# The v and o blocks of an mLSTM layer by Strassen's seven products, and x with the first weights in contiguous parts

## What is computed

```python
h = rmsnorm(x, norm1_g[l])
z = jnp.einsum('bsd,de->bse', h, w_in[l])
q_a, k_a, v_a, x_m, v_m, o_m, i_pre, f_pre = jnp.split(z, IN_SPLITS, axis=-1)
...                       # attention of q_a, k_a, v_a; convolution of x_m; mLSTM with v_m; sigmoid(o_m) as its gate
x = x + jnp.einsum('bse,ed->bsd', mixed, w_out[l])
x = x + moe_ffn(rmsnorm(x, norm2_g[l]), ...)   # every expert: [1024 x 2048], SwiGLU, [1024 x 1024]
```

## Time and profile before

| | us |
|---|---|
| median of 3 runs | 1050.03 (1049.18 to 1050.25) |
| the profiled execution | 1048.32 |
| its span, first to last instruction | 1046.5 |
| TensorE busy in the span | 1031.7 |
| VectorE busy | 199.1 |
| ScalarE busy | 143.0 |
| GpSimd busy | 4.1 |
| mean load rate over the span | 407 GB/s |

### The profile page before, as it was taken

The page is one execution under the profiler, slowest core; times in us unless marked ns, Lnnn a source line. Parts: engine busy times, 40 slices in busy tenths (PEclk is TensorE's granted clock), DMA queues, the critical chain, the costliest instruction groups (busy, mean ns, idle before and its releaser), DMA issues.

```text
span 1046.5 us, 11612 instructions
## 1 busy us (share of the span) xinstructions
PE 1031.7 (99%) x4797; PEld 385.9 (37%) x4797; DVE 199.1 (19%) x506; ACT 143.0 (14%) x301; POOL 4.1 (0%) x20
## 2 busy tenths in 40 slices
PE   8999999999999999999999999999999999999998
PEld 4655543333333333333333333333333333333333
DVE  1263232111111111111111111111111111111111
ACT  2144431100111100100111111111101100011101
POOL 0000000000000000000000000000000000000000
PEclk9999999999999999999999999999999999999999
DMA  9954799999999999999999999999999999999997
GB/s 341 428 217 161 292 364 406 427 428 434 432 429 431 431 432 431 433 431 432 433 431 432 430 433 431 432 431 432 435 431 433 430 432 425 431 426 427 424 425 292
DMA packets 24313, 425.87 MB, mean 407 GB/s; under 512 B 2912, under 2 KB 3424, under 8 KB 6368
## 3 DMA queue, kind: packets, MB, share of 16 engines
q1 hardware_dynamic: 23856, 424.96, 95.6%
q10 hardware_dynamic: 432, 0.55, 0.1%
HBM read 424.45 MB, written 1.05 MB: 407 GB/s over the span
## 4 chain that ended last, share of the span: by engine, by line
PE 87%; DMA 8%; SPq 5%; another core or an unknown queue 0%; DVE 0%; issue 0%; ACT 0%
PE bank L1607 38%; PE bank L1642 18%; PE bank L1211 6%; PE bank L1519 5%; PE bank L1569 5%; DMA ring<-in_w_gate_up 5%; SPq L422 3%; PE bank L1404 3%; PE bank L1457 3%; PE bank L1530 2%; DMA ring<-in_w_down 2%; PE bank L1627 2%; PE bank L1249 1%; DMA ring<-in_w_in 1%; PE bank L1618 1%; SPq L567 0%
## 5 line engine op out<-in xcount | busy, mean ns | idle before, releaser
L1607 PE MATMUL bank<-ring,xe_t 128*64 128x512 f32 x2048 | 447.9, 594 | 5.1 <-DMA ring<-in_w_gate_up 4.6
L1607 PEld LDWEIGHTS bank<-ring,xe_t 128*64 128x64 f32 x2048 | 143.8, 137 | 305.6 <-issue 293.8
L1642 PE MATMUL bank<-ring,late 128*64 128x512 f32 x992 | 219.9, 596 | 0.0
L1642 PEld LDWEIGHTS bank<-ring,late 128*64 128x64 f32 x992 | 68.4, 137 | 127.3 <-issue 122.0
L1144 DVE TENSOR_SCALAR gate_c<-bank 128x512 f32<-128x512 f32 x32 | 22.2, 692 | 432.1 <-PE bank L1607 432.1
L1211 PE MATMUL bank<-ring 128*128 128x512 f32 x160 | 73.5, 605 | 2.2 <-DVE ring L908 2.1
L810 ACT ACTIVATE s_sb<-bank 128x256 f32<-128x256 f32 x32 | 12.3, 384 | 454.8 <-PE bank L1618 454.8
L1569 PE MATMUL bank<-late,s_sb 64*128 64x512 f32 x248 | 61.6, 615 | 0.0
L1519 PE MATMUL bank<-xres,pick 128*64 128x512 f32 x248 | 60.1, 605 | 0.0
L826 ACT ACTIVATE late<-bank 128x512 f32<-128x512 f32 x31 | 18.5, 597 | 218.8 <-PE bank L1642 218.8
L1142 DVE COPY row_of<-fold 128x64 f32 x31 | 6.0, 195 | 197.0 <-PE bank L1457 197.0
(11 more groups left out here) (212 smaller groups left out, 421.2 us busy)
## 6 DMA issues: line engine op xcount, KB each, us to landing
ring<-in_w_gate_up SPq DMA_DIRECT2D x44, 4096.0 KB, 33.9
ring<-in_w_down SPq DMA_DIRECT2D x22, 4096.0 KB, 32.4
ring<-in_w_gate_up SPq DMA_DIRECT2D x36, 2048.0 KB, 32.9
ring<-in_w_down SPq DMA_DIRECT2D x15, 2048.0 KB, 11.7
ring<-in_w_in SPq DMA_DIRECT2D x5, 2048.0 KB, 22.3
ring<-in_w_gate_up SPq DMA_DIRECT2D x8, 1024.0 KB, 23.5
ring<-in_w_down SPq DMA_DIRECT2D x6, 1024.0 KB, 29.2
ring<-in_w_out SPq DMA_DIRECT2D x2, 2048.0 KB, 32.3
```

Source lines behind the costliest of these rows:

```text
L1607: mm = pe.matmul(bank[h][c * CAP:(c + 1) * CAP, :], xe_t[:, k, :], w[:, k % RUN, at:at + BANK], start=False, stop=(k == KD - 1), skip_grou ...
L1642: mm = pe.matmul(dst[c * CAP:(c + 1) * CAP, :], turned[:, at:at + CAP], w[:, k % DRUN, c * BANK:(c + 1) * BANK], start=(k == 0), stop=(k = ...
```

## The change

Both products of the filler become one: the tokens A (256 x 1024) times the v and o weights side by side, B (1024 x 1024), by Strassen's method. A and B are cut in 2 x 2 quarters (A: 128 x 512, B: 512 x 512), and seven quarter products of 4 matmuls each replace eight. VectorE makes four sums of A's quarters (`s_1` to `s_4`, 128 x 512 words), GpSimd four sums of B's quarters (`t_1` to `t_4`, 128 x 2048 words; `t_3` and `t_4` in place in the weights, `t_1` and `t_2` in slot 2 behind the x weights). The results are put together partly in PSUM (a product that starts with `start=False` adds to the one before) and partly by VectorE (`fill_added`, and one addition straight into `vm`). ScalarE's copies go from four to two. The fillers are 14 halves, placed by `FILL_AT`: 4, 4, 3 and 3 in the four passes, where it was 4 each.

The loads of slots 0, 2 and 1 for the experts now wait for `z_fill` 6 and 7, since slots 0, 1 and 2 are in use till then. The transposed tokens and block 0 of the weights come as one tensor, `first`, whose four parts are each contiguous in memory (x and weights of a k side by side, 3 KB a partition and k); they land in slots 5 and 6 and no longer in 9 and 0, so block 4 can be loaded into slot 0 without a wait. `attn_bias` and `w_out` are loaded later in SyncE's order.

```diff
-X_PARTS = ((0, 1), (1, 2), (2, 4), (4, KD))
+FIRST_PARTS = ((0, 1), (1, 2), (2, 4), (4, KD))
+FIRST_RUN = SEQ + HALF
+FILL_AT = (((0, 1), (2,), (3,)), ((4, 5), (6,), (7,)), ((8, 9), (10,), ()), ((11, 12), (13,), ()))
...
         sig_c = km_t
+        s_1 = in_second_half(4 * P).rearrange("p (k n) -> p k n", k=4)
+        s_2, s_3 = (qm_t[:, 2 * i:2 * i + 2, :].rearrange("p h (g n) -> p (h g) n", g=2) for i in range(2))
+        t_1, t_2 = (ring[:, 2 * PIECE + i * 4 * HALF:2 * PIECE + (i + 1) * 4 * HALF].rearrange("p (k n) -> p k n", k=4)
+                    for i in range(2))
+        b_11, b_21, b_12, b_22 = (win[:, c, 4 * r:4 * r + 4, :] for c in range(2) for r in range(2))
+        t_4, t_3 = b_11, b_12
...
-        xg = hn_flat.rearrange("p (k n) -> p k n", k=KD)
+        first_flat = ring[:, 5 * PIECE:5 * PIECE + KD * FIRST_RUN]
+        x_win = first_flat.rearrange("p (k n) -> p k n", k=KD)
+        xg, win_0 = x_win[:, :, 0:SEQ], x_win[:, :, SEQ:FIRST_RUN]
+        u_2 = hn_flat[:, HM * SW:T * D]
...
+        u_3 = ring[:, 9 * PIECE + T * D + 4 * SW:10 * PIECE]
...
+        a_11, a_12, a_21, a_22 = (ht[:, 4 * c:4 * c + 4, r * P:(r + 1) * P] for r in range(T) for c in range(2))
...
             def load_win(b):
-                sp.dma_start(win[:, b % WINS, :, :], w_in[b]).then_inc(ld_win[b], 16)
+                sp.dma_start(win[:, b % WINS, :, :], w_in[b - 1]).then_inc(ld_win[b], 16)
...
-            for i, (lo, hi) in enumerate(X_PARTS):
-                sp.dma_start(xg[:, lo:hi, :], x_t[:, lo:hi, :]).then_inc(ld_xt[i], 16)
-                sp.dma_start(win[:, 0, lo:hi, :], w_in[0, :, lo:hi, :]).then_inc(ld_xt[i] if i else ld_win[0], 16)
+            for i, (lo, hi) in enumerate(FIRST_PARTS):
+                rows = first[lo:hi].rearrange("k n -> (k n)").rearrange("(p n) -> p n", p=P)
+                sp.dma_start(first_flat[:, lo * FIRST_RUN:hi * FIRST_RUN], rows).then_inc(ld_first[i], 16)
...
+            sp.dma_start(wr_br, w_router).then_inc(ld_wr, 16)
+            load_win(4)
+            sp.wait_ge(z_q, 4)
+            load_win(5)
+            sp.wait_ge(h_ready, 2)
             sp.dma_start(bias_a, attn_bias).then_inc(ld_bias_a, 16)
-            sp.dma_start(wr_br, w_router).then_inc(ld_wr, 16)
...
-            for b in (4, 5):
-                sp.wait_ge(z_q, 2 * (b - WINS) + 2)
-                load_win(b)
-            for b, used, n in ((2, z_xm, 2), (3, z_v, 2), (0, z_fill, 2)):
-                sp.wait_ge(used, n)
-                load_gu(0, b, b)
-                if b == 2:
-                    for i in range(4):
-                        sp.dma_start(bgu[i * NE:(i + 1) * NE, :], b_gate_up[0, :, i * BANK:(i + 1) * BANK]).then_inc(ld_bgu, 16)
+            sp.wait_ge(z_v, 2)
+            load_gu(0, 3, 3)
+            for i in range(4):
+                sp.dma_start(bgu[i * NE:(i + 1) * NE, :], b_gate_up[0, :, i * BANK:(i + 1) * BANK]).then_inc(ld_bgu, 16)
...
-            sp.wait_ge(z_fill, 4)
+            sp.wait_ge(z_fill, 6)
+            load_gu(0, 0, 0)
+            load_gu(0, 2, 2)
+            sp.wait_ge(z_fill, 7)
...
+            for b in (4, 5):
+                pool.wait_ge(ld_win[b], 16)
+            pool.wait_ge(z_xm, 2)
+            pool.tensor_tensor(t_1, b_12, b_11, ALU.subtract).then_inc(t_ready, 1)
+            pool.wait_ge(t_ready, 1)
+            pool.tensor_tensor(t_2, b_22, t_1, ALU.subtract).then_inc(t_ready, 1)
+            pool.tensor_tensor(t_3, b_22, b_12, ALU.subtract).then_inc(t_ready, 1)
+            pool.wait_ge(t_ready, 2)
+            pool.wait_ge(z_fill, 1)
+            pool.tensor_tensor(t_4, b_21, t_2, ALU.subtract).then_inc(t_ready, 1)
...
             def filled(n):
-                act.wait_ge(z_fill, n + 1)
-                if n < 2:
-                    act.activation(vm[:, n, :, 0:DM], bank[n][:, :].rearrange("p (h n) -> p h n", h=HM),
+                if n == 0:
+                    act.wait_ge(z_fill, 1)
+                    act.activation(p_1, bank[0][:, :], ACT.Copy).then_inc(fill_read, 1)
+                if n == 1:
+                    act.wait_ge(z_fill, 3)
+                    act.activation(vm[:, 0, :, 0:DM], bank[0][:, :].rearrange("p (h n) -> p h n", h=HM),
                                    ACT.Copy).then_inc(fill_read, 1)
-                else:
-                    act.activation(om[:, n - 2, :], bank[n - 2][:, :], ACT.Copy).then_inc(fill_read, 1)
...
                                   bank[5][:, 0:SEQ].unsqueeze(1).broadcast_to([P, 4, SEQ]), ALU.mult).then_inc(h_ready, 1)
+            dve.wait_ge(h_ready, 2)
+            step(dve.tensor_tensor(s_1, a_21, a_22, ALU.add))
+            step(dve.tensor_tensor(s_3, a_11, a_21, ALU.subtract))
+            settle()
+            step(dve.tensor_tensor(s_2, s_1, a_11, ALU.subtract))
+            settle()
+            dve.tensor_tensor(s_4, a_12, s_2, ALU.subtract).then_inc(h_ready, 1)
...
+            def fill_added(out, held, product, b):
+                dve.wait_ge(z_fill, product)
+                dve.tensor_tensor(out, held, bank[b][:, :], ALU.add).then_inc(fill_sum, 1)
             for j in range(PAIRS):
+                if j == 1:
+                    dve.wait_ge(fill_read, 1)
+                    fill_added(u_2, p_1, 2, 1)
+                if j == 2:
+                    fill_added(u_3, p_1, 4, 1)
...
+                if j == PAIRS - 1:
+                    dve.wait_ge(z_fill, 6)
+                    dve.wait_ge(consts, 5)
+                    dve.tensor_tensor(vm[:, 1, :, 0:DM], p_1.rearrange("p (h n) -> p h n", h=HM),
+                                      bank[1][:, :].rearrange("p (h n) -> p h n", h=HM), ALU.add).then_inc(fill_sum, 1)
...
                 normalise(2 * j + 1)
+                if j == 2:
+                    dve.wait_ge(fill_sum, 2)
+                    fill_added(om[:, 1, :], u_3, 5, 0)
+                if j == PAIRS - 1:
+                    fill_added(om[:, 0, :], u_2, 7, 0)
...
                 for k in ks:
-                    mm = pe.matmul(dst[:, :], tokens[:, k, t * P:(t + 1) * P], win[:, b % WINS, k, :],
+                    mm = pe.matmul(dst[:, :], tokens[:, k, t * P:(t + 1) * P], win[:, b % WINS, k, :] if b else win_0[:, k, :],
...
-            pe.wait_ge(ld_win[0], 16)
-            for k in range(KD):
-                pe.wait_ge(x_norm, k + 1)
-                for t in range(T):
-                    mm = project(bank[t], 0, t, range(k, k + 1), xg)
-                    if k == KD - 1:
-                        mm.then_inc(z_q, 1)
+            for i, (lo, hi) in enumerate(FIRST_PARTS):
+                pe.wait_ge(ld_first[i], 16)
+                for k in range(lo, hi):
+                    pe.wait_ge(x_norm, k + 1)
+                    for t in range(T):
+                        mm = project(bank[t], 0, t, range(k, k + 1), xg)
+                        if k == KD - 1:
+                            mm.then_inc(z_q, 1)
...
+            fill_a = (a_11, s_2, a_12, s_3, s_1, a_22, s_4)
+            fill_b = (b_11, t_2, b_21, t_3, t_1, t_4, b_22)
+            fill_anew = (True, True, False, False, True, False, False)
...
-                b, t, q = 4 + i // 8, (i // 4) % 2, i % 4
+                n, q = i // 2, i % 2
                 if q == 0:
-                    if t == 0:
-                        pe.wait_ge(ld_win[b], 16)
-                    if b == 4:
-                        pe.wait_ge(v_read, t + 1)
-                    else:
-                        pe.wait_ge(fill_read, t + 1)
-                mm = project(bank[t], b, t, range(2 * q, 2 * q + 2))
-                if q == 3:
+                    if n == 0:
+                        pe.wait_ge(ld_win[4], 16)
+                        pe.wait_ge(v_read, 1)
+                    if n == 1:
+                        pe.wait_ge(v_read, 2)
+                        pe.wait_ge(h_ready, 3)
+                        pe.wait_ge(t_ready, 2)
+                    if n == 2:
+                        pe.wait_ge(fill_read, 1)
+                    if n == 3:
+                        pe.wait_ge(fill_sum, 1)
+                        pe.wait_ge(t_ready, 3)
+                    if n == 4:
+                        pe.wait_ge(fill_read, 2)
+                    if n == 5:
+                        pe.wait_ge(fill_sum, 2)
+                        pe.wait_ge(t_ready, 4)
+                    if n == 6:
+                        pe.wait_ge(fill_sum, 3)
+                for k in (2 * q, 2 * q + 1):
+                    mm = pe.matmul(bank[n % 2][:, :], fill_a[n][:, k, :], fill_b[n][:, k, :],
+                                   start=fill_anew[n] and k == 0, stop=(k == 3), skip_group_check=True)
+                if q:
...
                     pe.wait_ge(m_g, HM - 1 + h // 2)
-                    pe.wait_ge(fill_read, 3 + h // 2)
+                    if h == 0:
+                        pe.wait_ge(fill_read, 2)
+                        pe.wait_ge(fill_sum, 5)
...
                     attend(j - 1)
-                fill(4 * j)
-                fill(4 * j + 1)
```

(31 more changed lines are left out.)

## The result

The changed kernel takes 1057.44 us (median of 5 runs, 1056.47 to 1057.70), the kernel before, run beside it, 1049.18 us (5 runs, 1048.71 to 1050.25). The ratio is 1.0070, with a 95% interval of 1.0058 to 1.0082: slower by 8.3 us, where the forecast was a gain of 3.3. The profiled execution lasts 1057.51 us around a span of 1055.7.

What follows compares the result with a forecast made beforehand. The experts' load stream was taken to set the end, its start set by TensorE's line. First loads 2.4 plus seven products 1.9 minus GpSimd sums 1.0 gave 3.3 us, so 1046.7 us; range 1044.4 to 1056, the forecast's own 1045.2 to 1047.9.

Steps and rivals of the forecast that it cites:

- the cost of the sums on GpSimd: VectorE's convolution beside GpSimd's sums: slowed to end 3.8 us late, 2.9 hidden, so a cost of 1.0 us.
- VectorE keeps 62%: VectorE beside a running GpSimd sum: 0.09 us lost in 0.24 us of overlap, so it keeps 62% of its rate.
- the slack of 2.87: ScalarE's copies after the convolution end at 65.90 us, TensorE asks at 68.77: 2.87 us of lateness stays hidden.
- The port is held: Rival, chance 0.28: each GpSimd sum blocks VectorE's second input for its whole length, costing 8.7 us; 1054.4 us.
- Its other term: Within the held-port rival: t_4 catches normalise(1), 3.9 us late against 2.2 of slack, 1.7 us more.
- The first loads: Block 0 at the start: contiguous loads remove TensorE's gaps, gaining 2.4 us, bounds 0 and 2.6.
- Seven products: Fill stage: 28 matmuls instead of 32 save 3.44 us, less 1.5 us of waits, a gain of 1.9 us.
- both predicted waits: Pass 3, TensorE waiting behind VectorE's additions: 0.5 us at turn_p(6) and 1.0 us at m_sum(0).
- The moved loads: Slots 0, 2 and 1 loaded after z_fill 6 and 7: cost 0, the old pause pays, 1.9 us in hand.
- The 1-for-1 rule: Each microsecond by which TensorE reaches the first expert earlier moves the load stream and the end by as much.

Runs made afterwards that it cites:

- kept-busy kernel: The changed kernel with 36 unused products (72 records) on TensorE in its stall ahead of the gate columns; 1058.19 us, ratio 1.0088 to the kernel before.
- loads alone: The kernel before with only the contiguous first loads and the new place and load order that go with them, ordinary products, no weight sums; 1046.39 us, ratio 0.9973.
- sums early: The changed kernel with t_1 and t_2 made sooner in slot 10, t_3 after the gate rows, t_4 after a normalisation; 1045.92 us, ratio 0.9969 to before.
- kernel without sums: The changed kernel without GpSimd's four weight sums, its products reading unsummed weight quarters in the same number and order; 1045.73 us, ratio 0.9968 to before.
- reordered version: Sums early, with VectorE's two additions of pass 3 each moved one step later, behind what TensorE waits for; 1044.22 us, ratio 0.9949 to before.
- in parts: The changed kernel with each of its four GpSimd sums cut into four instructions of 512 elements; 1056.67 us, ratio 1.0066 to before.

## Why the prediction was wrong

**The step that failed** is the cost of the sums on GpSimd: "VectorE keeps 62%" and, from it, "Cost 1.0 us". The rate came from one copy of 0.29 us beside a select of 0.29 us, a pair too short to tell a share from a hold. In its place: the two engines take turns by whole instructions where both read SBUF. The convolution ended at 69.76 us, about 11.2 later than its old place shifted by the faster start (61.07 - 2.5), where the sum had 3.8. Less the slack of 2.87, which was right, that is the stall of 8.3 us for the forecast 1.0. The low clock behind it, some 3.6 us, had no term in the sum at all.

**The rival had the mechanism and not the size.** "The port is held" said 1054.4, 4.4 us slower than before; 8.3 were measured. That it is a port that is held, no run here shows; that VectorE is held for whole instructions, they do. It had one VectorE instruction let in between two sums, as the trace shows, and 3.9 us a sum; 4.5 were measured. Three sums of 0.6 more would have made its stall 7.0 + 1.8 = 8.8, where 8.3 were measured. What it lacked altogether is the clock behind the stall, 3.2 to 3.6 us. Its other term, 1.7 us for t_4 on normalise(1), is real (2.2 us in the kept-busy kernel) but did not show, since the low clock had moved t_4. And I gave it 0.28 for want of a row of two two-input instructions side by side. The rule that spoke for it, in "SBUF — State Buffer" of the Trainium skill, section "Who interferes with whom", is borne out by 3.17 us instead of 0.42; so are the 4.5 us for a sum of 2048 words of the "GPSIMD Engine Reference", section "Performance versus the Vector engine" (4.52).

**The first loads** were expected to give 2.4 us. The changed kernel's profile has 2.48, and alone they gave 2.3 by the medians (1048.73 - 1046.39). The spread starts at 25.7 to 28.1 us in the ten kernels with the new loads, 2.3 us earlier than 29.04 on average, so a single profile can be 1.3 us off here. The profile of loads alone is the latest of them, at 28.07.

**Seven products.** The mechanism is right: 28 products, and both predicted waits, at the predicted instructions (0.65 and 0.92 in the idle column, for 0.5 and 1.0). The gain was expected at 1.9 us. From the gate columns to the output product the kernel before takes 46.33 us and sums early 44.95: 1.4. The idle column hides part of the waits, since the end of a record is modelled. By the starts in the changed kernel, L1356 follows the filler of 112.04 by 2.53 us instead of four records of 0.43, 0.8 late, and L1429 (the `m_sum` of the changed kernel) follows the three turns of 117.99 (0.33) by 1.40, 1.1 late: 1.9 of waits, not 1.5.

**The moved loads** were costed at nothing. In the changed kernel TensorE was so late that this was no test. The kernel without sums has the same loads, and TensorE reaches the experts 3.1 us sooner than before; in sums early and the reordered version it does so 3.8 and 5.9 us sooner. In all three the end follows within about 1.4 us, so at most that much is theirs. The load rate speaks against it: without sums the old pause (180 and 90 GB/s at 142 to 146 us before) is nearly gone, at 349 and 276 GB/s in 140 to 144, but the dip where the first expert lets the next load go is still there (287 GB/s in 152 to 154, 197 in 156 to 158 before), so the loads ahead of it had landed. What the up to 1.4 us are stays open.

**The 1-for-1 rule**, that the end moves with the first expert, held to within about 1.4 us from profile to profile. That +8.25 in the profile stands beside +8.26 in the median is partly luck, since the spans of the same two profiles differ by 9.2.

## What to carry to other kernels

Before work goes to GpSimd "because it is idle", list what VectorE does in those microseconds with operands in SBUF, and count the two engines as one: the sum of their times, wherever they overlap. The price is then set by the moment and not by the amount; the same sums cost 11 us or nearly nothing (0.2 against no sums), with the first two six microseconds earlier and the third behind the gate rows. And a long stall of TensorE can cost more than its length: the ones of 7.6 to 8.4 us did, while a stall of 2.2 us in the kernel kept busy left the granted clock at 1.00.

## What was unexpected of the hardware

- **One-input instructions are held too.** The taps of L992 have one tensor input and went from 0.35 us each to 9.77 for four. Those that read PSUM were not held (0.48 us). The held ones read SBUF and are also faster, 0.35 us for 256 elements against 0.48 from PSUM; the trace cannot tell which of the two decides. "SBUF — State Buffer" of the Trainium skill, same section, has this case: a tensor_scalar in a mode that uses both ports contends. The trace agrees in that they were held, and normalise(1), 4.87 us for two, is a second case; the mode itself it does not show.
- **Turns are strict.** One VectorE instruction passed between two GpSimd ones, whether these took 4.5 us or, in parts, about 1.2 (16.12 us for twelve with VectorE's between them).
- **The clock's tail.** TensorE idle from about 66.3 to 74.6 us had a granted clock of 0.58 in 68 to 70, 0.50 from 70 to 82, and 1.00 after, with TensorE at work again since 74.6. Kept busy with unused products it stayed at 1.00, and 3.2 to 3.5 us came back.
